# Gates of one dense tile: indirect scatter-adds into a DRAM table in place of one-hot products

## The reference, cut

```python
def one(xb):                                     # PEER_HEADS 8, PEER_NKEYS 128, PEER_TOPK 16
    q = (xb @ w_query).reshape(T, PEER_HEADS, 2, PEER_DKEY // 2)
    s = jnp.einsum('thpd,phkd->thpk', q, sub_keys).astype(jnp.float32)
    sv_, si = lax.top_k(s, PEER_TOPK)
    cand = (sv_[:, :, 0, :, None] + sv_[:, :, 1, None, :]).reshape(...)
    cand_idx = (si[:, :, 0, :, None] * PEER_NKEYS + si[:, :, 1, None, :]).reshape(...)
    top_s, pos = lax.top_k(cand, PEER_TOPK)
    idx = jnp.take_along_axis(cand_idx, pos, axis=-1)
    g = jax.nn.softmax(top_s, axis=-1)
    act = jax.nn.gelu(jnp.einsum('td,thkd->thk', xb, expert_u[idx]).astype(jnp.float32))
    return jnp.einsum('thk,thkd->td', (g * act).astype(xb.dtype), expert_v[idx])
```

## Time and profile before

| | us |
|---|---|
| median of 3 runs | 1970.55 (1962.52 to 1974.61) |
| profiled execution | 1968.53 |
| its span, first to last instruction | 1966.7 |
| TensorE busy | 1849.2 (94%) |
| VectorE busy | 1381.5 (70%) |
| ScalarE busy | 858.6 (44%) |
| GpSimd busy | 580.2 (30%) |

### The profile page before, as it was taken

One profiled execution on the slowest core, in us unless ns is written; L12 is line 12 of the kernel. 1 busy time (PEld: TensorE's weight loads), 2 busy tenths in 40 slices (PEclk: granted clock), 3 DMA queues, 4 the chain that ended last, 5 costly groups with the idle time before them and its releaser, 6 DMA issues.

```text
span 1966.7 us, 28631 instructions
## 1 busy us (share of the span) xinstructions
PE 1849.2 (94%) x11094; PEld 1640.0 (83%) x11094; DVE 1381.5 (70%) x2538; ACT 858.6 (44%) x1167; POOL 580.2 (30%) x441
## 2 busy tenths in 40 slices
PE   7999988897999999999999999997899999999996
PEld 2799976687999999999989999997677777777774
DVE  4532354536439887879878798785778888888757
ACT  1222244412115545555545545553455555555552
POOL 0111100001110145323553346434445554443100
PEclk9999999888999999999999999998899999999998
DMA  8543332031204699899999999999989998999641
GB/s 285 188 170 129 105 132 81 1 102 49 86 22 131 203 318 373 284 312 305 346 325 314 303 321 344 334 324 386 347 333 391 358 385 346 403 355 385 271 187 68
DMA packets 184522, 496.83 MB, mean 253 GB/s; under 512 B 12908, under 2 KB 75976, under 8 KB 171976
## 3 DMA queue, kind: packets, MB, share of 16 engines
q1 hardware_dynamic: 129096, 293.72, 41.8%
q0 software_dynamic: 55296, 201.35, 27.7%
HBM read 443.90 MB, written 51.12 MB: 252 GB/s over the span
## 4 chain that ended last, share of the span: by engine, by line
PE 74%; DVE 13%; DMA 7%; ACT 3%; issue 1%; POOL 1%; SPq 0%; DVEq 0%; ACTq 0%
PE PS L1000 22%; PE PS L548 11%; PE PS L550 11%; PE PS L549 11%; PE PS L612 4%; PE PS L947 4%; DMA gat<-in_peer_v_dram,idx 3%; DMA vrw<-in_peer_v_dram 2%; PE PS L921 2%; PE PS L573 1%; DVE gat L1771 1%; DMA gat<-in_peer_u_dram,idx 1%; DVE vl L1907 1%; DVE acc L1792 1%; POOL gat L1430 1%
## 5 line engine op out<-in xcount | busy, mean ns | idle before, releaser
L1430 POOL DMA_INDIRECT gat<-in_peer_v_dram,idx x192 | 273.2, 1423 | 329.0 <-DVE acc L1792 295.5
L1430 POOL DMA_INDIRECT gat<-in_peer_u_dram,idx x192 | 247.6, 1290 | 404.0 <-DVE a L1771 330.2
L548 PE MATMUL PS<-XH,uth 128*128 128x352 f32 x1024 | 341.8, 334 | 0.0
L549 PE MATMUL PS<-XL,uth 128*128 128x352 f32 x1024 | 330.5, 323 | 0.0
L550 PE MATMUL PS<-XH,utl 128*128 128x352 f32 x1024 | 330.2, 322 | 0.0
L1000 PE MATMUL PS<-vh,wh 128*128 128x512 f32 (+1 forms) x768 | 244.4, 399 | 18.0 <-DVE vl L1907 9.1
L1792 DVE SCALAR_TENSOR_TENSOR acc<-gat,a,acc 128x1024 f32<-128x1024 f32 x185 | 235.5, 1281 | 34.3 <-DMA gat<-in_peer_v_dram,idx 32.4
L1771 DVE CUSTOM_DVE_ANT_0 gat<-gat,x 128x1024 f32<-128x1024 f32 x192 | 231.0, 1221 | 27.9 <-DMA gat<-in_peer_u_dram,idx 27.7
L548 PE MATMUL PS<-XH,whi 128*128 128x272 f32 x784 | 231.3, 295 | 14.9 <-DVE XL L1718 8.3
L1000 PE MATMUL PS<-vl,wh 128*128 128x512 f32 (+1 forms) x768 | 241.0, 395 | 0.0
L1000 PE MATMUL PS<-vh,wl 128*128 128x512 f32 (+1 forms) x768 | 239.9, 393 | 0.0
(11 more groups left out here) (288 smaller groups left out, 3249.7 us busy)
## 6 DMA issues: line engine op xcount, KB each, us to landing
uraw<-in_peer_u_dram SPq DMA_DIRECT2D x128, 512.0 KB, 5.7
vrw<-in_peer_v_dram SPq DMA_DIRECT2D x64, 1024.0 KB, 7.1
acts_dram<-gel SPq DMA_DIRECT2D x128, 176.0 KB, 6.3
gates_dram<-gst SPq DMA_DIRECT2D x22, 1024.0 KB, 10.4
al<-acts_dram SPq DMA_DIRECT2D x16, 1408.0 KB, 10.2
G<-gates_dram SPq DMA_DIRECT2D x16, 1408.0 KB, 14.5
adaw<-in_w_ada_dram SPq DMA_DIRECT2D x8, 2048.0 KB, 8.0
wraw<-in_w_in_dram SPq DMA_DIRECT2D x7, 2048.0 KB, 7.8
```

The lines of the kernel that those rows point to most:

```text
L548: mm(out, ah, bh, start=start, stop=False)
L549: mm(out, ah, bl, start=False, stop=False)
L1430: nc.gpsimd.indirect_dma_start(out=gat[:, n % NGAT, :], out_offset=None, in_=table, in_offset=bass.IndirectOffsetOnAxis(ap=idx[:, k:k + 1] ...
```

## The change

Tile 2 leaves the one-hot path. A table in DRAM, `tile_gates` (128 x 16 x 128 x 8 float32), is filled with zeros by one DMA on SP from a zeroed buffer of 4 KB a partition, which GpSimd sets behind its casts for the last projection. `choose(2)` makes for each chosen expert of each token the place in the table (`idxs`, six more VectorE instructions) and keeps the gates in `gs`. GpSimd then issues 128 indirect DMAs that add 128 elements of 4 bytes each into the table, two behind each fetch from fetch 60 on; within 16 of them the places of a token differ, and before each further 16 it waits until the ones before have landed. The down loop loads `G` in two parts, the first 128 tokens from the table and the other 224 from `gates_dram`. `one_hot`, `sel_turn`, `gates`, `gates_out` and eight `gate_store` of tile 2 are gone.

With it the schedule by hand moves: `choose(1)` has one dot behind each step (it had none) and `choose(2)` to `choose(4)` one instead of two; the scores of tiles 3 and 4 come at m = 30 and 46 and no longer wait for gates; the gates of tile 3 start at m = 55 and those of tile 4 at 90; the gelu of the sparse tiles stands at 121; there are 28 early weighs instead of 22; the first loads of `al` and `vrw` are spread over m = 100 to 118, the first of `G` is at 124. Near the end of the down loop the product for tile 1 (`s_mix4`), `residual(1)`, `normed` and `deviation` move by one to three j. Some semaphores of the norms are merged by name only.

```diff
-NGT = TD // OG
-NBLK = TD // TB
+NGT = (TD - P) // OG
+NBLK = (TD - P) // TB
...
-EXP_AT = (2, 10, 26, 61, 100)
-SEL_AT = (0, 0, 33, 70, 109)
-GATE_AT = (0, 0, 35, 72, 110)
-GATE_PER = (0, 0, 2, 2, 2)
-SCORE_AT = (0, 0, 8, 46, 84)
-GELU_AT = 108
-FILL = (0, 0, 2, 2, 2)
-FILL_HOT = (0, 0, 1, 1, 1)
-EARLY = 22
+EXP_AT = (2, 11, 24, 45, 80)
+SEL_AT = (0, 0, 0, 53, 88)
+GATE_AT = (0, 0, 0, 55, 90)
+GATE_PER = (0, 0, 0, 2, 2)
+SCORE_AT = (0, 0, 8, 30, 46)
+GELU_AT = 121
+FILL = (0, 1, 1, 1, 1)
+FILL_HOT = (0, 0, 0, 1, 1)
+SCATTER_FROM = 60
+SCATTER_PER = 2
+EARLY = 28
+ACT_LOADS = (100, 104)
+V_LOADS = (114, 118)
...
+        def gate_load(c):
+            if c >= 2:
+                sp.wait_ge(s_wv, JB * (c - 1))
             if c < 2:
                 sp.wait_ge(s_gout[0], 16 * (NBLK // 2))
                 sp.wait_ge(s_gout[1], 16 * (NBLK // 2))
+                sp.wait_ge(s_scat, 16 * P)
             if c == 1:
                 sp.wait_ge(s_up, NU)
-            sp.dma_start(G[c % 2][:], gates_d[:, c]).then_inc(s_g[c % 2], 16)
+            sp.dma_start(G[c % 2][:, 0:P], tile_gates[:, c]).then_inc(s_g[c % 2], 16)
+            sp.dma_start(G[c % 2][:, P:TD], gates_d[:, c]).then_inc(s_g[c % 2], 16)
+
+        sp.wait_ge(s_qz, 2)
+        sp.dma_start(tile_gates.rearrange("p b t j -> p b (t j)"), bc(zeros[:], 1, NJB)).then_inc(s_zeroed, 16)
         sp.wait_ge(gemms[2].lo, 16)
         u_load(0)
         u_load(1)
...
             pe.wait_ge(s_scev, SCORES[i])
-            if i >= 3:
-                pe.wait_ge(s_gev, NG * (i - 2) - gates_left(i - 1))
...
-            if j == NU - 8:
+            if j == NU - 5:
                 pe.wait_ge(s_tke, 8)
                 pe.wait_ge(s_dot, 2 * NSP)
...
         gemm_hi(gemms[2])
+        pool.wait_ge(s_glo, 5)
+        nc.gpsimd.memset(zeros[:], 0.0).then_inc(s_qz, 1)
...
+        def scatter():
+
+            k = scattered[0]
+            if k == P:
+                return
+            scattered[0] += 1
+            if k == 0:
+                pool.wait_ge(s_zeroed, 16)
+                pool.wait_ge(s_sel, 3)
+            elif k % TOPK == 0:
+                pool.wait_ge(s_scat, 16 * k)
+            nc.gpsimd.indirect_dma_start(out=gates_flat, out_offset=bass.IndirectOffsetOnAxis(ap=idxs[:, k:k + 1], axis=0),
+                                         in_=gs[:, k:k + 1], in_offset=None, compute_op=ALU.add).then_inc(s_scat, 16)
...
+            if n >= SCATTER_FROM:
+                for _ in range(SCATTER_PER):
+                    scatter()
...
+            if i == 2:
+                whole, part = posa.rearrange("p h k -> p (h k)"), posf[:, 0].rearrange("p h k -> p (h k)")
+                after(nc.vector.tensor_copy(whole, sel[:, 1, :]))
+                after(ts(whole, whole, 3, None, ALU.logical_shift_right))
+                after(nc.vector.tensor_copy(part, whole))
+                after(stt(part, part, float(P * JB - JB), sel[:, 1, :], ALU.mult, ALU.add))
+                after(stt(part, sel[:, 0, :], float(NJB * P * JB), part, ALU.mult, ALU.add))
+                after(ts(idxs[:], part, cst[:, C_TOK:C_TOK + 1], None, ALU.add))
...
-            one_hot(i)
+            if i >= 3:
+                one_hot(i)
...
             if j == NU - 11:
                 residual(0)
-            if j == NU - 7:
+            if j == NU - 4:
                 residual(1)
-            if j == NU - 3:
                 normed(0)
+            if j == NU - 1:
                 normed(1)
```

More of the change, by code:

```diff
@@ L88, in shape_constants @@
     small[:, C_IOTA:C_IOTA + P] = i[None, :]
+    small[:, C_TOK] = JB * i
     log_g = np.log1p(-np.exp2(-5.0 - np.arange(NH)))
@@ L124, in build @@
     cst = at("cst", 0, [C_N])
-    o = 4 * C_N + 16
+    o = 4 * C_N + 12
     ones = at("ones", o, [P])
@@ L202, in build @@
     negI = at("negI", 5632, [P], F32R)
+    idxs = at("idxs", place["negones"], [P], U32)
+    gs = at("gs", place["meanw"], [P])
     low = Region(R0, R0 + 49152)
@@ L245, in build @@
     skraw = at("skraw", place["gst"], [16, P])
+    zeros = at("zeros", place["gst"] + 12288, [P * JB])
     late = Region(RP, RP + 16 * 4 * T)
@@ L322, in build @@
         st = Stage()
-        st.sq, st.ss, st.sd, st.tmp, st.y, st.hi, st.lo = (
-            sem(f"s_n{n}_{x}") for x in ("sq", "ss", "sd", "tmp", "y", "hi", "lo"))
+        st.sq, st.ss, st.sd, st.scaled, st.hi, st.lo = (
+            sem(f"s_n{n}_{x}") for x in ("sq", "ss", "sd", "scaled", "hi", "lo"))
         norms.append(st)
@@ L353, in build @@
     s_gt = sem("s_gt")
+    s_zeroed, s_scat = sem("s_zeroed"), sem("s_scat")
     s_oh, s_gmm, s_gev = sem("s_oh"), sem("s_gmm"), sem("s_gev")
@@ L372, in build @@
     acts = act_dram.rearrange("p u t -> p (u t)")
-    gates_d = gate_dram.rearrange("p b t j -> p (b t j)")[:, 0:NJB * TD * JB].rearrange(
-        "p (b t j) -> p b t j", b=NJB, t=TD)
+    gates_d = gate_dram.rearrange("p b t j -> p (b t j)")[:, 0:NJB * (TD - P) * JB].rearrange(
+        "p (b t j) -> p b t j", b=NJB, t=TD - P)
+    tile_gates = nc.dram_tensor("tile_gates_dram", (P, NJB, P, JB), F32, kind="Internal").ap()
+    gates_flat = tile_gates.rearrange("p b t (j o) -> (p b t j) o", o=1)
     u_d = peer_u[0].rearrange("(p j) d -> p j d", p=P)
@@ L515, in _ @@
                 stored += 1
-            if m == NU - 5:
-                v_load(0)
+            if m in ACT_LOADS:
+                act_load(ACT_LOADS.index(m))
+            if m in V_LOADS:
+                v_load(V_LOADS.index(m))
             if m == NU - 4:
[L519 to L522, removed]
+                gate_load(0)
+        assert stored == NBLK, stored
         act_store(NU - 2)
         act_store(NU - 1)
-        block_load(1)
+        gate_load(1)
         for j in range(NU):
@@ L529, in _ @@
             if j % JB == 1 and 2 <= j // JB + 1 < NU // JB:
-                block_load(j // JB + 1)
+                act_load(j // JB + 1)
+                gate_load(j // JB + 1)
         for n in range(5):
@@ L939, in gates @@
         def gates(i, g):
-            gi = NG * (i - 2) + g
+            gi = NG * (i - 3) + g
             if gi >= 2:
                 pe.wait_ge(s_gev, gi - 1)
-            pe.wait_ge(s_scev, SCORES[i + 2 if i < 4 and g >= NG - gates_left(i) else i + 1])
+            pe.wait_ge(s_scev, SCORES[5])
             pe.wait_ge(s_oh, gi + 1)
@@ L953, in sel_turn @@
             pe.wait_ge(s_sel, i + 1)
-            pe.wait_ge(s_scev, SCORES[i + 1])
+            pe.wait_ge(s_scev, SCORES[5])
             for c in range(3):
@@ L969, in _ @@
             up(m, 1)
-            for i in range(2, 5):
+            for i in range(3, 5):
                 if m == SEL_AT[i]:
@@ L1128, in _ @@
         for k in range(KD):
-            act.wait_ge(norms[0].y, 2 * k + 2)
+            act.wait_ge(norms[0].scaled, 2 * k + 2)
             act_(XH[:, k, :], scr1[:, k, :], ACT.Copy).then_inc(norms[0].hi, 1)
@@ L1245, in _ @@
         for k in range(KD):
-            act.wait_ge(norms[1].tmp, 2 * k + 2)
+            act.wait_ge(norms[1].scaled, 2 * k + 2)
             for g, cols in enumerate((slice(0, TP), slice(TP, T))):
@@ L1283, in sel_out @@
         def sel_out(i):
-            act.wait_ge(s_selT, i - 1)
-            if i >= 3:
-                act.wait_ge(s_oh, NG * (i - 2))
+            act.wait_ge(s_selT, i - 2)
+            if i >= 4:
+                act.wait_ge(s_oh, NG * (i - 3))
             act_(selT[:], PS[:, 6, 0:3 * P].rearrange("p (c t) -> p c t", c=3), ACT.Copy).then_inc(s_selTe, 1)
@@ L1372, in _ @@
                 token_rows(j - 2)
-            if j == NU - 5:
+            if j == NU - 6:
                 deviation(0)
+            if j == NU - 2:
                 deviation(1)
@@ L1557, in _ @@
                 ts(scr1[:, k, cols], scr2[:, k, cols], coefA[:, 0, k, g:g + 1], modT[:, k, g:g + 1], ALU.mult,
-                   ALU.add).then_inc(norms[0].y, 1)
+                   ALU.add).then_inc(norms[0].scaled, 1)
             if k == 5:
@@ L1723, in _ @@
                 stt(scr2[:, k, cols], hT[:, k, cols], coefA[:, 1, k, g:g + 1], rs[:, cols], ALU.mult, ALU.mult
-                    ).then_inc(norms[1].tmp, 1)
+                    ).then_inc(norms[1].scaled, 1)
             if k >= 2:
@@ L1980, in gate_done @@
 def gate_done(gi):
-    i, g = 2 + gi // NG, gi % NG
+    i, g = 3 + gi // NG, gi % NG
     return GATE_AT[i] + g // GATE_PER[i]
```

20 lines of the change are left out of this document (10 added, 10 removed).

## The result

The changed kernel takes 2087.61 us (median of 4 runs, 2084.85 to 2094.65) beside 1970.97 us for the kernel before: ratio 1.0598, interval 1.0572 to 1.0625. The profiled execution has a span of 2083.8 us against 1966.7, 117.1 us more. Slower was right; the size was not: 1999 was forecast, 2051 was the upper end of the range.

What follows compares the result with a forecast made beforehand. TensorE, busy 94% of the span, was taken to set the pace. Terms -28.5 - 7 + 20 + 20 + 23 + 3 = +30.5 us on the profiled 1968.5 us gave 1999 us, range 1962 to 2051.

Steps and rivals of the forecast that it cites:

- gates of tile 2, late selection of tile 3: Up loop: 32 groups of gates at 0.89 us leave TensorE, -28.5 us; tile 3's selection no longer late, -7 us.
- zeroing ahead of turn(0): Start of up loop: u_load(0) queues on SP behind the 8.39 MB zeroing, so turn(0) waits: 17 us plus 3 for clock, +20.
- dots in choose(1), S: Dots behind choose(1)'s steps free S 15 us later for tile 2's scores; with 5 for clock +20, bounds 10 and 24.
- scatters, tile 3's gates: One_hot(3): fetches with two scatters each come slower than its dots are wanted, so TensorE waits: +23 us.
- scatters, choose(4) late: Choose(4) stretches by 10 to 15 us, which sel_turn at m = 88 leaves room for; no loss.
- end of the up loop: Before the first down product: 28 EARLY weighs end last, 59 us after m = 121 against 54 today: +3 us.
- down loop: 22 more weighs fill VectorE's slack, G's two loads carry the same bytes: 0, at most +5 us.
- rival 4: Zeroing writes slowly, at gst's 10.4 us for 1 MB: turn(0) waits 73 us, 2055 us in all; chance 0.07.
- rival 2: u_load(0) passes the zeroing, packets taking turns: no wait at turn(0), 1979 us; chance 0.05 alone.
- I take 4.7: Pace in us of a fetch with two scatters on GpSimd, each priced like a gather; estimates were 5.0 and 4.4.
- 26 paces + 9 − 107.6: Loss in one_hot(3): last of 27 rows beyond five fetched ahead, less the 107.6 us its 31 dots allow; +23 us.
- Rival 3: Scatter-adds hold up the gathers' queue, since each reads and writes: pace 6.7 us, loss 75, 2051 us; chance 0.12.

Runs made afterwards that it cites:

- after: The changed kernel as described under The change, against the kernel before; 2087.61 us (median of 4 runs), ratio 1.0598.
- plain scatters: The changed kernel with its 128 scatters writing over the places in the table instead of adding to them; 2038.06 us.
- one per fetch: The changed kernel with one scatter behind each fetch from fetch 60 on instead of two, so over 128 fetches instead of 64; 2049.86 us.
- the later scores: The changed kernel with tile 2's scores at m = 12 instead of 8 and the exponentials of tiles 1 and 2 at 14 and 27; 2076.62 us.

## Why the prediction was right in sign and wrong in size

Its steps against the ledger, in us; measured is after's stretch less that of before or its own work, and the first row is only what is left of the 117.1:

| step | predicted | measured |
|---|---|---|
| gates of tile 2, late selection of tile 3 | −28.5 − 7 | −39.6, as what is left |
| zeroing ahead of turn(0) | +20 | +14.2 |
| dots in choose(1), S | +20 | +14.4 |
| scatters, tile 3's gates | +23 | +51.7 |
| scatters, choose(4) late | 0 | +28.2 |
| u late, m 102 to 121 | 0 | +10.6 |
| end of the up loop | +3 | −0.1 |
| down loop | 0 | +37.7 |
| sum | +30.5 | +117.1 |

86.6 us are missing from the forecast: 37.7 in the down loop, 28.7 in the fetches' pace, 28.2 in choose(4) and 10.6 in m 102 to 121, less 18.6 by which other terms were too high. With the measured loss of tile 3's gates alone the sum would be 2028, still in the range; the down loop and choose(4), both put at nothing, took the time out of it. That slower was right was not luck: the zeroing, S and tile 3's gates, each seen in its place, make 80.3 us, more than twice the 39.6 that went away.

**The zeroing and S** went as told. The wait is 15.2 us, the write at 357 GB/s lies between the 338 and 420 from which 17 was taken; gst's pace (rival 4) and the passing u_load (rival 2) are out. The 207 GB/s that the Trainium skill (DMA: Bandwidth & Descriptors, Latency and other measured facts) gives for rows 512 KiB apart does not show at 64 KiB. The copy to S waits 17.7 us for the dots, "18 to 20" was told; 5 us for the clock behind it were too many.

**The scatters: the formula held, its size did not.** The step that failed is "I take 4.7", and in it "two scatters" at a gather's length. With the measured pace the prediction's own sum, 26 paces + 9 − 107.6, comes close to what these runs show; the pace here is that from fetch 78 to fetch 104, the span that it speaks of:

| kernel | pace | by the formula | measured in m 54–71 |
|---|---|---|---|
| after | 5.65 | 48.3 | 51.7 |
| plain scatters | 4.97 | 30.6 | 27.7 |
| one per fetch | 4.20 | 10.6 | 10.5 |

Only in after is this pace GpSimd's alone (in 146.9 us it waits 0.9 us for anything else); in the other two it waits 17 and 30 us of the stretch for dots, so there the pace is in part a result. And the formula needs its start of five rows ahead: with the later scores, where TensorE is at m = 54 15 us sooner but the fetches only 7, it gives 48.3 for a pace of 5.65, and 60.4 was measured.

A gather at 1.27, two scatter-adds at 1.79 and three gaps of 0.30 make 5.75 us. Rival 3, a pace of 6.7 and 2051 us, was the right mechanism by half of its reason: a scatter-add is longer than a gather, but on the issuing engine; its landing, which the prediction feared and priced at 0.7 us a fetch, cost 6.4 us in 64 fetches. Of the 51.7, TensorE was idle 34.8 (its waits at L963, above); the other 17 fall in with a lower granted clock, 0.78 to 0.93 between 960 and 1060 us, so partly 1.2 instead of 2.4 GHz, as behind the stalls of the earlier trace rows.

**choose(4)** was a second step that failed: "Choose(3) and choose(4) stretch by 10 to 15 us; sel_turn at 53 and 88 leaves that much". Choose(3) stretched by 25 us (107, against 82 without scatters, where 81 was told) and still came in time. Choose(4) stretched by 45, and it starts only when the late one_hot(3) is done. The prediction added up each stall at its own place and let no stall push the next due time; this one did.

**The down loop** was costed at nothing, "G comes in two loads with the same bytes". Of its 37.7 us the split is about 15 (tried on before), and 25 with the place of the table (tried on after). That VectorE's slack would take 22 more weighs was right; the remaining 10 us or so aren't explained.

**The blocks of u in m 102 to 121** (10.6 us) were not in the sum: the prediction saw the earlier loads only as the end of a wait. The loss stands without scatters too (8.6), but with one scatter behind each fetch it is 0.9, with the same loads. Where TensorE waits for u (1300 to 1340 us of after) the DMA engines move 386 to 418 GB/s, gathers among it; with one scatter behind each fetch they move 290 to 336 there. No experiment singled this out, and the cause stays open.

**The end of the up loop** came out at nothing: the EARLY weighs still end last (22.0 us of wait, L1016 on vl), as told.

## What to carry to other kernels

Price an indirect DMA first by the time that it holds its issuing engine, and look whose instructions are queued behind it there: 128 of them were 229 us on an engine that had to fetch for others every 3.5 us. Replacing 28 us of a full engine's work pays only if the other engine's cost fits into its slack in that very stretch, and if no later due time hangs on what slips. One large load and two small ones with the same bytes were not the same here, beside a busy second queue.

## What the runs showed of the hardware that I had not expected

- An indirect scatter of 128 elements of 4 bytes held GpSimd for 1.79 us in the mean with addition and 1.18 without it, a gather of 128 rows of 4 KB for 1.27 and 1.21 in the same two kernels: the addition makes the difference, not the bytes, which are 1000 times as many in the gather.
- Adding into DRAM element by element was not slow to land: 6.4 us of waits for 128 scatters, five stalls. The DMA engines were busy for a share of 0.76 to 0.84 meanwhile, with half the bytes of a full stretch.
- A DMA of 1.4 MB split into 0.9 and 0.5 MB cost the loop around it about 1 us for each of its 16 uses (14.8 us), and the transfer queued behind it landed 1.0 us later.
- A write of 8.39 MB from a 4 KB buffer repeated 16 times a partition went at 357 GB/s, faster than the loads of the earlier trace rows behind one another (338).
